# Prompt attention of a hybrid decoder step: scores with the keys on the partitions instead of the queries

## The chip, the cores and the metric

The kernel runs on one core of a Trainium2 chip. The metric is device microseconds (us) of one execution. TensorE (PE) multiplies, ScalarE (ACT), VectorE (DVE) and GpSimd (POOL) do the element-wise work, SyncE (SP) and POOL issue most DMAs. All arithmetic is on fp32 data; where a product needs full precision at the fast rate, an operand is split into a rounded high part (type fp32r) and a low part, and the product is made of several matmuls that add up in PSUM.

## The reference, cut to what matters

One decoder layer is computed for a prompt of 1024 tokens and for 8 samples of 8 tokens. Three head groups share one input projection: a sparse attention group (8 query heads, 2 KV heads, head size 64), a retention group, and a memory group (4 heads over 256 memory tokens). The change touches only the attention of the prompt:

```python
def masked_softmax(s, mask):
    s = jnp.where(mask, s.astype(jnp.float32), NEG_INF)
    m = jnp.max(s, axis=-1, keepdims=True)
    e = jnp.where(mask, jnp.exp(s - m), 0.0)
    return e / jnp.maximum(jnp.sum(e, axis=-1, keepdims=True), 1e-30)
...
    # per block of 128 queries and KV head (4 query heads each):
    s = jnp.einsum('bqkgd,bckd->bkgqc', q, kc) * SCALE      # compressed blocks (63 keys)
    s = jnp.einsum('bqkgd,bkqsd->bkgqs', qb, kg) * SCALE    # selected blocks (here all causal keys)
    s = jnp.einsum('bqkgd,bskd->bkgqs', qb, kw) * SCALE     # sliding window of 512 keys
    return gb[:, :, 0] * o_c + gb[:, :, 1] * o_s + gb[:, :, 2] * o_w
def mem_attend(q, mkv):
    s = jnp.einsum('bqhd,bmhd->bhqm', q, mkv[:, :, 0]) * SCALE
    p = jax.nn.softmax(s.astype(jnp.float32), axis=-1)
```

With 16 selected blocks of 64 keys and a prompt of 1024 tokens, the selected branch is plain causal attention. So a tile of 128 queries, number i (0 to 7), has i+1 key tiles of 128 in the selected branch, min(i+1, 5) in the window branch, one of compressed keys, and two of memory tokens.

## The kernel before, in words

The kernel has three stages on PE. The first projects the inputs (`pe_trunk`, lines 541 to 543) and slips compression, retention and the set-up of the attention between the projection jobs. The second is `pe_attend` with the prompt attention, into which the attention of the samples is slipped. The third (`project`, lines 1746 to 1748) multiplies the mixed heads by the output weights, a tile of 128 tokens at a time; its first step (lines 1742 and 1743, the samples) runs before the attention's last products.

The order of everything in the second stage is one list, made by `schedule()`, and each engine walks it in that order. Its unit v is one head of one query tile in one branch pair, `UNITS[v]`; there are 144. For a unit the list holds

- `qk`: PE adds the mask (line 1567, an identity by the mask, bf16) and the scores, with the queries as the stationary operand and the keys as the moving one: `QA` (high part of the queries, line 1575) and `QB` (low part, line 1576). The key tile `KS` has the keys' high part on the 64 partitions of its KV head and the low part on the other 64, and the queries stand on both halves, so the two matmuls give all four products. Scores lie in two pairs of PSUM banks, so `qk` of v waits for the exponentials of v-2 (line 1553);
- `max`: DVE reduces each row of scores to its negated maximum (line 1907);
- `sm`: ACT makes the exponentials with that maximum as bias and adds up each row (line 1839, two records: the operation and the read of its accumulator) into `P`;
- chunks `("p", ...)`: PE turns four tiles of 128 keys of `P` (line 1602, transposes) into one of three PSUM banks, 4, 5 and 6, which all small work shares in turn; ACT and DVE alternate in copying them to `PTs` (line 1772);
- `pv`: PE multiplies the values by `PTs` (line 1727), two heads of the two KV heads side by side, each on 64 columns of the array. An fp32 matmul leaves two records in the trace;
- `ot`, chunk `("o", ...)`, `norm`: ACT copies the output out of bank 7 (line 1863), PE turns it back (line 1607), DVE scales it by gate and sum (line 1929), POOL adds the branches (`pool_mix_group`).

Queries of later tiles are loaded by SP (`load_q`), turned by PE (line 1612), scaled by ACT or DVE into `qd` and split by POOL into `QA` and `QB` (lines 2142 and 2144). Chunks of the samples' attention (`sample_groups()`) follow one group to a unit. A chunk waits until the chunk three before it has been read (line 1592), since it takes its bank.

## Time and profile before

| | before |
|---|---|
| times of three runs, us | 970.45, 971.74, 973.53 (median 971.74) |
| span of the profiled execution, us | 970.0 |
| PE busy, share of the span | 96% |
| DVE, ACT, POOL busy, share of the span | 53%, 39%, 30% |
| granted TensorE clock, mean | 0.996 of full speed |
| PE records | 7997 |

The span runs from the first to the last instruction of the profiled execution, 1.7 us less than the median. A matmul's record is longer than the time it takes from the next one, since matmuls overlap in the array. What one costs is therefore read from the starts in the timeline, not from its duration.

### The profile page before, as it was taken

Reading aid. Unit: us, or ns where it says so; the run is one execution under the profiler, and the core shown is the slowest. Engines: PE = TensorE matmul, PEld = TensorE weight load, DVE = VectorE, ACT = ScalarE, POOL = GpSimd, SP = SyncE. Lnnn points to the kernel's source line nnn. Section 1 sums busy time; section 2 is a strip of 40 time slices with the busy share of each in tenths; the row PEclk is TensorE's granted clock in tenths of the full one; section 3 lists DMA queues with packets and bytes.
Section 4 is the critical chain, followed back from the end, with each engine's and each line's share of the span. In section 5 each row is a group of like instructions: output and inputs, shape, how many; then the busy total and the mean of one; then the engine's idle time right before and its main releaser. Section 6 shows DMA issues by size and latency. Waiting matters only on the chain.

```text
span 970.0 us, 20909 instructions
## 1 busy us (share of the span) xinstructions
PE 928.3 (96%) x7997; PEld 843.0 (87%) x7997; DVE 517.3 (53%) x1216; ACT 382.5 (39%) x973; POOL 289.1 (30%) x493
## 2 busy tenths in 40 slices
PE   4999999999999999999999999999999999999997
PEld 4999999999999999999988788878878888778885
DVE  6675322322222444337546677676777758944443
ACT  6333221224211012212456565656665657832221
POOL 0222222211216353462153153315311535310000
PEclk9999999999999999999999999999999999999998
DMA  7664404224242533322966156714504132424331
GB/s 242 157 218 117 158 20 170 84 100 118 69 142 83 134 127 100 104 82 60 226 191 146 36 155 240 240 44 123 167 2 126 56 103 73 134 98 134 132 133 69
DMA packets 97878, 119.16 MB, mean 123 GB/s; under 512 B 37763, under 2 KB 79779, under 8 KB 97203
## 3 DMA queue, kind: packets, MB, share of 16 engines
q1 hardware_dynamic: 84498, 74.41, 26.8%
q0 software_dynamic: 10224, 36.20, 11.0%
q10 hardware_dynamic: 3056, 7.21, 2.1%
q8 instruction: 65, 1.06, 0.5%
q14 instruction: 35, 0.28, 0.1%
HBM read 92.72 MB, written 32.02 MB: 129 GB/s over the span
## 4 chain that ended last, share of the span: by engine, by line
PE 78%; DVE 8%; issue 4%; DMA 4%; ACT 2%; POOL 2%; SPq 2%; DVEq 0%; ACTq 0%
PE psum L541 9%; PE psum L542 9%; PE psum L543 9%; PE psum L1727 7%; PE psum L1602 5%; PE psum L1575 3%; PE psum L1746 3%; PE psum L1747 3%; PE psum L1748 3%; PE psum L1576 3%; PE psum L770 2%; PE psum L772 2%; PE psum L771 2%; PE psum L753 2%; DMA r_rt<-in_c_rope 2%
## 5 line engine op out<-in xcount | busy, mean ns | idle before, releaser
L541 PE MATMUL psum<-a_whi,f_xhi 128*128 128x256 f32 (+1 forms) x864 | 250.9, 290 | 8.1 <-DVE f_xlo L959 4.4
L542 PE MATMUL psum<-a_wlo,f_xhi 128*128 128x256 f32 (+1 forms) x864 | 245.1, 284 | 0.0
L543 PE MATMUL psum<-a_whi,f_xlo 128*128 128x256 f32 (+1 forms) x864 | 244.3, 283 | 0.0
L541 PEld LDWEIGHTS psum<-a_whi,f_xhi 128*128 128x128 f32 x864 | 164.1, 190 | 11.9 <-issue 3.1
L543 PEld LDWEIGHTS psum<-a_whi,f_xlo 128*128 128x128 f32 x864 | 164.1, 190 | 0.0
L542 PEld LDWEIGHTS psum<-a_wlo,f_xhi 128*128 128x128 f32 x864 | 164.0, 190 | 0.0
L1907 DVE TENSOR_REDUCE p_nb<-psum 128x1 f32<-128x640 f32 (+7 forms) x224 | 110.4, 522 | 48.8 <-PE psum L1576 46.8
L1839 ACT ACTIVATE p_P<-psum,p_nb 128x640 f32<-128x640 f32 (+7 forms) x224 | 124.3, 562 | 25.9 <-DVE p_nb L1907 23.5
L685 POOL DMA_DIRECT2D h_scratch<-a_hst x117 | 64.1, 550 | 234.7 <-DVE a_hst L1015 146.4
L1602 PE MATMUL psum<-f_ident,p_P 128*128 128x128 f32 x656 | 101.8, 279 | 3.0 <-ACT p_qd L1852 1.4
L1602 PEld LDWEIGHTS psum<-f_ident,p_P 128*128 128x128 f32 x656 | 74.0, 140 | 8.6 <-ACT p_qd L1852 1.9
L1024 DVE TENSOR_TENSOR c_ctlo<-psum,c_cthi 128x512 fp32r<-128x512 f32 (+1 forms) x40 | 25.4, 636 | 101.1 <-ACT c_cthi L914 101.1
L1772 ACT COPY p_PT<-psum 128x512 f32<-128x512 f32 (+3 forms) x105 | 48.1, 458 | 66.1 <-PE psum L1602 65.3
L1727 PE MATMUL psum<-p_PT,p_V 128*64 128x128 f32 x1056 | 71.8, 279 | 1.5 <-DVE p_PT L1772 0.6
L1575 PE MATMUL psum<-p_KS,p_QA 128*128 128x320 f32 (+5 forms) x192 | 72.0, 378 | 0.0
L914 ACT CAST c_cthi<-psum 128x512 fp32r<-128x512 f32 (+1 forms) x40 | 21.8, 544 | 119.4 <-PE psum L753 119.4
L1727 PEld LDWEIGHTS psum<-p_PT,p_V 128*64 128x64 f32 x1056 | 56.4, 136 | 12.4 <-issue 9.5
L1772 DVE COPY p_PT<-psum 128x512 f32<-128x512 f32 (+3 forms) x111 | 64.5, 582 | 0.2
L1576 PE MATMUL psum<-p_KS,p_QB 128*128 128x320 f32 (+5 forms) x192 | 62.1, 327 | 0.0
L1746 PE MATMUL psum<-d_whi,d_xh 128*128 128x512 f32 x128 | 51.2, 400 | 0.0
L530 DVE TENSOR_TENSOR a_wlo<-a_wraw,a_whi 128x1024 fp32r<-128x1024 f32 (+1 forms) x30 | 37.7, 1294 | 24.8 <-ACT a_whi L523 24.7
L1747 PE MATMUL psum<-d_wlo,d_xh 128*128 128x512 f32 x128 | 50.6, 396 | 0.0
(317 smaller groups left out, 1836.6 us busy)
## 6 DMA issues: line engine op xcount, KB each, us to landing
a_wraw<-in_w_in SPq DMA_DIRECT2D x24, 512.0 KB, 4.9
h_scratch<-a_hst POOLq DMA_DIRECT2D x96, 128.0 KB, 2.6
s_SG<-in_cache_nsa_slc SPq DMA_DIRECT2D x64, 128.0 KB, 2.3
a_xraw<-in_x_prompt SPq DMA_DIRECT2D x8, 512.0 KB, 3.7
p_qd<-h_scratch SPq DMA_DIRECT2D x16, 256.0 KB, 4.0
s_MK<-in_cache_mem SPq DMA_DIRECT2D x8, 512.0 KB, 9.8
s_WG<-in_cache_nsa_win SPq DMA_DIRECT2D x8, 512.0 KB, 4.7
mix_scratch<-p_zt POOLq DMA_DIRECT2D x8, 512.0 KB, 3.8
```

Source lines behind the costliest of these rows:

```text
L541: nc.tensor.matmul(out, hi, wh, start=first, stop=False)
L542: nc.tensor.matmul(out, hi, wl, start=False, stop=False)
L543: return nc.tensor.matmul(out, lo, wh, start=False, stop=last)
L1575: nc.tensor.matmul(o, QA[par[i]][:, hq, :], k, start=at // 512 not in masked, stop=False, skip_group_check=True)
L1576: l = nc.tensor.matmul(o, QB[par[i]][:, hq, :], k, start=False, stop=True, skip_group_check=True)
L1602: l = nc.tensor.transpose(o[0:w, 128 * j:128 * j + 128], P[v % 2][:, at:at + w], ident[:])
L1727: i_mm = nc.tensor.matmul(psum[64 * j:64 * j + 64, at:at + 128], val, PTs[p_rank[pair[j]] % NPT][0:w, 128 * p:128 * p + 128], start=k == 0 ...
L1746: nc.tensor.matmul(o, hi, dwhi[jj][:, k], start=k == 0, stop=False)
L1747: nc.tensor.matmul(o, hi, dwlo[jj][:, k], start=False, stop=False)
L1772: copy(PTs[r % NPT][0:w, 0:128 * n], bank(4 + c % 3)[0:w, 0:128 * n]).then_inc(sem, 1)
L1839: nc.scalar.activation(dst, s_view(s), ACT.Exp, bias=nb[:, g % NNB:g % NNB + 1], accum_out=ssum[:, par[i], s[1]:s[1] + 1]).then_inc(S("p_e ...
L1907: nc.vector.tensor_reduce(out=nb[:, g % NNB:g % NNB + 1], in_=s_view(s), op=ALU.max, axis=AX.X if len(s[6]) == 1 else AX.XY, negate=True). ...
```

## The change

The unit of the attention stage becomes a block of one query tile and one KV head (16 blocks, `BLOCKS`), walked in the order of tiles 0, 2, 4, 6, 7, 5, 3, 1. For each block there are now two passes over the scores:

- a pass for the maxima alone, one block ahead: 9 units (`qk`, `max`), with masks as before and the `QA` matmuls alone. DVE reduces them into columns of `nbm`; chunk `("m", n)` turns `nbm` once, and ACT copies the rows of negated maxima into the unused half of the low part of the queries, `QB`, four copies;
- the scores themselves, turned: chunk `("s", n, b, k)` has 128 keys as the stationary operand and the 4 query heads (512 columns) as the moving one, `KS` by `QA` and then `KB` by `QB`. `KB` holds the keys' high part on one half and on the other half a constant that is one in the row of that branch's maximum. So the second matmul adds both the low part and the negated maximum. Where a mask is needed a third matmul adds it. ACT makes the exponentials from the shared bank straight into `PTs`, with no row sum. The transposes of `P`, `P` itself and the copies to `PTs` go.

The row sums come from the probabilities: POOL adds up the tiles of the selected branch (`A_s`), DVE those of the window branch (`A_w`), each add a 128x512 fp32 operation, and chunk `("u", n)` multiplies them by one-hot columns (`esel`), 20 products of 32 array columns each. Chunk `("v", n)` turns the result for DVE's weights. `pv` now takes 256 columns to a matmul instead of 128.

Queries are split by ACT and DVE straight from the bank, three deep. The memory layout moves: the values `V` and `VM` now lie where the projection's inputs were, so their load is issued after the projection has been stored, ahead of the loads of the third and fourth block's queries and of the samples' inputs; the masks are loaded first. In the set-up the keys are copied twice by ACT (`KS`, `KB`), and POOL fills `KB`'s constant rows. The output stage's weights are split in 8 pieces of 256 KB loads instead of 4 of 512 KB, and its residual rows and `gf` are loaded when the attention's last products are done.

```diff
-    PAIRS = [(6, 1), (7, 0), (5, 2), (4, 3)]
-    BLOCKS = [(pair[j], g) for pair in PAIRS for j, g in ((0, 0), (0, 1), (1, 0), (1, 1), (0, 2), (1, 2), (1, 3), (1, 4), (0, 3), (0, 4))]
+    TILES = [0, 2, 4, 6, 7, 5, 3, 1]
+    BLOCKS = [(i, kv) for i in TILES for kv in range(2)]
+    UNITS = [(n, l) for n in range(NB) for l in range(9)]
...
@@ def schedule():
+        for n in range(NB):
+            mine = score_chunks(n)
+            span = len(mine) - 2 if len(mine) >= 6 else len(mine) - 1
+            units = [list(range(9 * (n + 1) + 9 * k // span, 9 * (n + 1) + 9 * (k + 1) // span)) if n + 1 < NB and k < span else [] for k in range(len(mine))]
...
+            for k, c in enumerate(mine):
+                if k == len(mine) - 1 and n + 1 < NB:
+                    add(("m", n + 1))
+                pending.append(add(c))
+                due = [p for p in pending if p <= pending[-1] and len(pending) - pending.index(p) > 2]
+                if due and ends_phase(due[0]):
+                    products(1)
+                elif len(due) >= 2:
+                    products(2)
                 else:
+                    follow()
+                for v in units[k]:
+                    unit(v)
+                if n + 2 < NB and k in (1, 2):
+                    add(("q", n + 2, k - 1))
+                    if k == 2 and n + 4 < NB:
+                        steps.append(("load_q", n + 4))
...
@@ def sp_attend(sp):
-        load_q(sp, SECOND)
         wait_stored(sp, len(proj_jobs) - 1)
...
+        sp.dma_start(esel[:], io["c_esel"]).then_inc(S("p_esel"), 16)
+        for br, c in enumerate((C_KVS, C_KVW)):
+            sp.dma_start(V[:, br], hD[0:T, c + 128:c + 256].rearrange("(t p) n -> p t n", p=128)).then_inc(S("p_v"), 16)
+        sp.dma_start(VM[:], new_mem[:, 256:512].rearrange("(t p) n -> p t n", p=128)).then_inc(S("p_v"), 16)
+        load_q(sp, 2)
+        load_q(sp, 3)
...
@@ def qk(v):
-            if v >= 2:
-                pe.wait_ge(S("p_exp"), sm_count(v - 2))
+            else:
+                pe.wait_ge(S("p_nb"), max_count(v - 2))
...
-                    nc.tensor.matmul(o, QA[par[i]][:, hq, :], k, start=at // 512 not in masked, stop=False, skip_group_check=True)
-                    l = nc.tensor.matmul(o, QB[par[i]][:, hq, :], k, start=False, stop=True, skip_group_check=True)
-            l.then_inc(S("p_qk"), 1)
+                    r = nc.tensor.matmul(psum[:, at:at + w], QA[n % 3][:, hq, :], k, start=at // 512 not in masked, stop=True, skip_group_check=True)
+            r.then_inc(S("p_qk"), 1)
+
+        def scores(c, o):
...
+            if (b, k) == (0, 0):
+                wait_queries(pe, n)
+                wait_chunk_read(pe, place["m", n])
+            if b == 3:
+                for hh in range(2):
+                    for m in range(2):
+                        om, keys = o[:, 128 * (2 * hh + m):128 * (2 * hh + m) + 128], slice(128 * m, 128 * m + 128)
+                        nc.tensor.matmul(om, KM[:, kv + 2 * hh, keys], qa[:, 4 + hh, :], start=hh + m == 0, stop=False, skip_group_check=True)
+                        l = nc.tensor.matmul(om, KMB[:, kv + 2 * hh, keys], qb[:, 4 + hh, :], start=False, stop=True, skip_group_check=True)
+                return l
...
+            og = o.rearrange("p (g q) -> p g q", g=4)
+            if m_at is not None:
+                nc.tensor.matmul(og, maskb[:, m_at:m_at + 128], identb[:].rearrange("p (o q) -> p o q", o=1).to_broadcast([128, 4, 128]), start=True, stop=False)
+            nc.tensor.matmul(og, ka, qa[:, 0:4, :], start=m_at is None, stop=False)
+            return nc.tensor.matmul(og, kb, qb[:, 0:4, :], start=False, stop=True)
+
+        def sums(n, o):
...
+            for b in range(4):
+                p = (A_s, A_w)[b] if b < 2 and summed(n, b) else probs(chunk_of(n, b, first_key(i, b)))
+                for m in range(2 if b == 3 else 1):
+                    for t in range(4):
+                        at = 256 * (t % 2) + 128 * m if b == 3 else 128 * (2 * (t % 2) + t // 2)
+                        l = nc.tensor.matmul(o[32 * t:32 * t + 32, 0:128], esel[:, 32 * b:32 * b + 32], p[:, at:at + 128],
+                                             start=b == 0, stop=b == 3 and m == 1, skip_group_check=True)
...
@@ def act_attend(act):
+                if kind[0] == "s":
+                    act.wait_ge(S("p_tr"), n + 1)
+                    if s_rank[n] >= NPT:
+                        wait_probs_read(act, s_index[s_rank[n] - NPT])
+                    nc.scalar.activation(probs(n)[:], o, ACT.Exp).then_inc(S("pt_act"), 1)
+                elif kind[0] == "m":
...
+                    rows = slice(64 - 64 * kv, 68 - 64 * kv)
+                    for g in range(4):
+                        src = psum[32 * g:32 * g + 4, 512 * (4 + n % 3):512 * (4 + n % 3) + 128]
+                        if g < 2:
+                            k = nc.scalar.copy(QB[m % 3][rows, g::4, :], src.rearrange("p (o q) -> p o q", o=1).to_broadcast([4, 2, 128]))
+                        else:
+                            k = nc.scalar.copy(QB[m % 3][rows, g, :], src)
```

## Rows read from the trace of the kernel before

**Rows 1.** The page's part 1: busy time, share of the span, records.
```profile
PE 928.3 (96%) x7997; PEld 843.0 (87%) x7997; DVE 517.3 (53%) x1216; ACT 382.5 (39%) x973; POOL 289.1 (30%) x493
```

**Rows 2.** Windows, the three stages: length, busy (records) by engine, clock, DMA.
```profile
0.00:489.00 489.00, 467.88 (x3905) 457.17 (x3906) 205.56 (x477) 125.62 (x233) 146.34 (x240) 1.00 0.42 125
489.00:867.00 378.00, 364.48 (x3654) 307.95 (x3654) 267.25 (x623) 233.83 (x680) 135.84 (x241) 1.00 0.41 122
867.00:970.00 103.00, 95.95 (x442) 77.92 (x441) 44.51 (x116) 23.00 (x60) 6.88 (x13) 0.98 0.32 115
```

**Rows 3.** Lines of PE from 489 to 867 us: busy, mean ns | idle before.
```profile
L1602 PE MATMUL psum<-f_ident,p_P 128*128 128x128 f32 x656 | 101.8, 279 | 3.0 <-ACT p_qd L1852 1.4 <-DVE p_PT L1772 1.0 <-ACT s_PTS L1790 0.4
L1575 PE MATMUL psum<-p_KS,p_QA 128*128 128x320 f32 (+5 forms) x192 | 72.0, 378 | 0.0
L1727 PE MATMUL psum<-p_PT,p_V 128*64 128x128 f32 x1056 | 71.8, 279 | 1.5 <-DVE p_PT L1772 0.6 <-issue 0.6
L1576 PE MATMUL psum<-p_KS,p_QB 128*128 128x320 f32 (+5 forms) x192 | 62.1, 327 | 0.0
```

**Rows 4.** Timeline of PE at 558 us: start, us, line, form, records.
```profile
558.03 0.45 PE L1575 MATMUL psum<-p_KS,p_QA 128*128 128x448 f32 x1
558.31 0.36 PE L1576 MATMUL psum<-p_KS,p_QB 128*128 128x448 f32 x1
558.51 0.37 PE L1575 MATMUL psum<-p_KS,p_QA 128*128 128x448 f32 x1
...
558.92 0.60 PE L1602 MATMUL psum<-f_ident,p_P 128*128 128x128 f32 x4
559.45 0.66 PE L1727 MATMUL psum<-p_PT,p_V 128*64 128x128 f32 x8
559.94 0.39 PE L1727 MATMUL psum<-p_PT,f_VC 128*64 128x128 f32 x4
560.26 0.66 PE L1612 MATMUL psum<-f_ident,p_qd 128*128 128x128 f32 x4
```

**Rows 5.** Timeline of PE in the output stage.
```profile
899.80 0.40 PE L1746 MATMUL psum<-d_whi,d_xh 128*128 128x512 f32 x1
900.03 0.39 PE L1747 MATMUL psum<-d_wlo,d_xh 128*128 128x512 f32 x1
```

**Rows 6.** Timeline of PE, products on 32 array columns, and what follows.
```profile
553.80 0.40 PE L1650 MATMUL psum<-s_MK,s_PTM 128*32 128x256 f32 x4
554.13 0.39 PE L1575 MATMUL psum<-p_KM,p_QA 128*128 128x256 f32 x1
```

**Rows 7.** Lines of ACT, DVE and POOL (489 to 867 us; the first two from 640 us).
```profile
L1839 ACT ACTIVATE p_P<-psum,p_nb 128x512 f32<-128x512 f32 x16 | 11.1, 693 | 1.9 <-DVE p_nb L1907 1.9
L1772 ACT COPY p_PT<-psum 128x256 f32<-128x256 f32 x19 | 7.1, 372 | 13.8 <-PE psum L1602 13.7
L1839 ACT ACTIVATE p_P<-psum,p_nb 128x640 f32<-128x640 f32 (+7 forms) x224 | 124.3, 562 | 25.9 <-DVE p_nb L1907 23.5 <-PE psum L1602 0.8 <-PE psum L1581 0.6
L1907 DVE TENSOR_REDUCE p_nb<-psum 128x1 f32<-128x640 f32 (+7 forms) x224 | 110.4, 522 | 48.8 <-PE psum L1576 46.8 <-ACT p_P L1839 0.7
L1772 DVE COPY p_PT<-psum 128x512 f32<-128x512 f32 (+3 forms) x111 | 64.5, 582 | 0.2
L2037 DVE TENSOR_TENSOR d_wlo<-d_wraw,d_whi 128x1024 fp32r<-128x1024 f32 x8 | 10.6, 1319 | 0.2 <-ACT d_whi L1883 0.2
L2144 POOL TENSOR_TENSOR p_QB<-p_qd,p_QA 128x512 fp32r<-128x512 f32 x21 | 26.8, 1277 | 1.7
```

**Rows 8.** Set-up and start: key copies, first exponential, query loads (KB, us to landing).
```profile
L950 ACT CAST p_KS<-psum x8: 579/582/585, 466.8 to 473.3; 64x512 fp32r<-64x512 f32 x8
...
494.35 0.99 ACT L1839 ACTIVATE p_P<-psum,p_nb 128x896 f32<-128x896 f32 x1
...
p_qd<-h_scratch SPq DMA_DIRECT2D x8, 256.0 KB, 5.0
```

**Rows 9.** Source of line 2088, a POOL addition: ns min/median/max.
```profile
L2088 POOL TENSOR_TENSOR p_Oi<-p_Oi x32: 452/457/1394, 514.1 to 867.4; 128x128 f32<-128x128 f32 x32
```

More of the change, by code:

```diff
@@ new lines, in follow @@
+        def follow():
+            if queue:
+                c = queue.pop(0)
+                add(c)
+                if c[0] == "o" and c[2] == 1:
+                    steps.append(("norm", c[1]))
+                    i, kv = BLOCKS[c[1]]
+                    if kv == 1:
+                        nxt = TILES.index(i) + 2
+                        if nxt < QT:
+                            timed.append([2, ("load_z", TILES[nxt])])
+                            timed.append([6, ("gates", TILES[nxt])])
@@ L1369, in schedule @@
             if d == 0:
-                while waiting:
-                    pv()
-                while outs:
-                    write(outs.pop(0)[0])
+                while pending:
+                    products(2 if len(pending) >= 2 and not ends_phase(pending[0]) else 1)
+                while queue:
+                    follow()
+                steps.extend([("load_x", 0), ("load_x", 1)])
             if d + 2 < NT:
@@ L1910, in weights @@
[L1910 to L1913 removed]
+            if l == 0 and n >= 1:
+                dve.wait_ge(S("p_tr"), place["m", n - 1] + 1)
+            for b, g, _, views in maxes(v):
+                nc.vector.tensor_reduce(out=nbm[:, 32 * g + b:32 * g + b + 1], in_=max_view(views), op=ALU.max, axis=AX.X if len(views) == 1 else AX.XY,
+                                        negate=True).then_inc(S("p_nb"), 1)
```

851 lines of the change are left out of this document (444 added, 407 removed).

## The prediction

> **What bounds the kernel now.** Read the busy shares first [rows 1]: PE is busy 96% of the span, DVE 53%, ACT 39%, POOL 30%. Then the windows by stage [rows 2]: the change acts on the middle one, 489 to 867 us, where PE is busy 364.5 of 378 us at the full clock (1.00) while DVE has 267, ACT 234 and POOL 136. So the stage is set by the number and form of matmuls, and at most 13.5 us of it is idle time that a better order could give back. A lighter DVE or ACT gives nothing beyond that. The lines of PE [rows 3] show what the change touches: transposes of P (656), score matmuls (192 wide ones by QA, as many by QB), values (1056 records of V). Their durations overlap, so prices come from the distance of starts.
>
> **Prices.** In [rows 4] a QB matmul of 448 columns takes 558.51 - 558.31 = 0.20 us, a QA of as many columns behind a mask 0.28, four transposes 0.53 before the value products begin and value records of 128 columns 0.49 for eight. With 0.11 for a transpose (4 x 0.11 = 0.44) that leaves 0.09 for the change of form into value products; the last four records take 0.32 against some 0.22 to 0.24, so 0.10 for the change back. In [rows 5] a matmul of 512 columns takes 0.233 us, its stationary operand's load hidden. In [rows 6] four records on 32 columns each of the array, 256 wide, take 0.33 us with the change of form, 0.23 without: they run side by side.
>
> **Removed from PE.**
> - QB in the score pass: 288 matmuls. 192 for V's branches and 32 for memory have 75,800 columns (528 x 128 + 32 x 256), at 0.20/448 us each 34 us. 64 compressed ones are only 64 wide; they can't be shorter than the load of a stationary operand, for which I take the transpose's 0.11: 7 us. Together 41 us.
> - 656 transposes x 0.11 = 72 us.
> - Value products: columns stay the same (two matmuls of 256 for four of 128), so 0 (bounds: -5 from fewer records, +3). They come in about 84 groups plus 16 of sums instead of 116; 16 fewer changes of form x 0.19 = 3 us less.
>
> **Added to PE.**
> - Turned scores. The number of chunks: selected branch 36, window 30, compressed and memory 8 each, times two KV heads = 164. 148 of them are two matmuls of 512 columns: 148 x 0.466 = 69 us. The 16 memory chunks are eight matmuls of 128 columns with a stationary operand each, 0.11 apiece: 14 us. 56 chunks have a mask (16 + 16 diagonals, 8 window tails, 16 compressed), 512 columns of it: 56 x 0.233 = 13 us. Entering the form: between 0 and 0.08 a chunk (0.28 against 0.20 in [rows 4]), half the chunks follow work of the same form; I take 4 us of at most 13.
> - Sums: 20 fp32 products a block are 40 records, ten sets of four. A set of 256 columns takes 0.23 [rows 6]; at 128 columns half of it, 0.12, is what the array rate leaves, 0.23 the other bound. With 0.2 for changes of form 16 x 1.4 = 22 us (bounds 18 and 40).
> - 32 transposes of maxima and sums: 4 us.
> - The pass of the maxima keeps masks and QA: no change.
>
> Added 69 + 14 + 13 + 4 + 22 + 4 = 126, removed 41 + 72 + 3 = 116: **PE's own work grows by 10 us** (bounds -5 and +35). The transposes' saving is eaten because the score products are now made one and a half times and the sums are PE's.
>
> **The other engines.** ACT: before 234 us; after, 164 exponentials x 0.69 (128x512 in [rows 7], without the accumulator reads) = 113, four copies a block at 0.37 = 24, output and query copies 34, sums 4, the rest some 35 as now: 210. DVE: 267 - 65 (copies to PTs) - 7 + 44 window adds at half of 1.32 us, 29 + query splits 15 = 240; the 224 maxima stay [rows 7]. POOL: 136 - 40 (splits) + 56 adds x 1.28 [rows 7] = 72 + 7 for wider mixing = 175. All far below PE's some 385, so they are hidden as long as their order holds. PE now never waits for a maximum before an exponential, since that lies a block ahead, and probabilities reach the values three chunks later. Of the 13.5 us idle I take 10 as given back (bounds: all of it, and 15 us more than before).
>
> **The start.** Three things are exposed there.
> - Set-up: ACT makes ten more key copies at 0.58 us [rows 8], 5.8 us inside some three projection jobs, with evictions queued behind them that PE needs four jobs later, and the key loads now land behind the mask's. Cover: the projection. I take 2 us (0 to 5).
> - First block: nothing can be scored until nine units are reduced (14 reduces, some 4 us), turned, copied four times (1.5 us). The first exponential, at 494.35 [rows 8] today, comes some 6.5 us later. In these 6.5 us PE has the units' 2.5 us of matmuls, which are not extra work, and about 1 us of idle time that it has today as well; 3 us are new (1 to 5).
> - The third block's queries are turned one chunk after the first scores, but SP issues their load behind V and VM (1.25 MB), and only when the projection is stored. A load of queries lands 5.0 us after its issue [rows 8]. PE stops at that chunk, and all chunks are behind it: 4 us (0 to 9).
>
> Nine us together. The values load is needed later than these queries and hides. The late load of residual rows has the second output step, 48 x 0.233 = 11 us, as cover; if it were gone it would cost the load's 5 us. The query loads of later blocks have two blocks of cover.
>
> **The sum.** Span 970.0 + 10 - 10 + 9 = 979. The median of the runs is 1.7 us over the span of the profiled execution, so 980.7 us.
>
> **Rivals.**
> 1. *The order heals it.* The added side work is small beside what ACT and DVE lose (65 us of copies, 45 of accumulator reads), so all 13.5 idle us go; forms of matmul cost nothing to enter (-4), value records gain 5, and the queries land in time, leaving 3 us at the start. For it: PE's idle gaps end mostly at ACT and DVE. Against: a stage with 96% of PE already busy. 970 + 10 - 13.5 - 4 - 5 + 3 = 960.5, 962 us measured. Chance 0.27.
> 2. *ACT becomes the pace at the block seams (slower still).* Every score bank is now read by ACT alone, out of three shared banks, and at each seam ACT has the four copies of maxima (1.5 us) before the next block's scores may start, with output, sum and query copies queued in the same place. It decides once ACT's queue at a seam exceeds the one score chunk and value pair that PE has there (0.9 + 0.5 us). Price 1.3 us x 16 on top of the forecast: 20 us, 1000 us. Speaks against it that ACT has only 210 us in 164 chunks, 1.3 us for PE's 2.3. A relative of it: a POOL addition usually takes 0.46 us but once 1.39 [rows 9], so POOL can be held up threefold, and its adds free the probability buffers. If each of the 44 window adds held or was held for one POOL add, 44 x 1.28 = 56 us would fall on DVE, which has 138 us free, so by itself it moves nothing. Chance 0.12 for both. The Trainium skill (SBUF — State Buffer, section Who interferes with whom) says that DVE and GpSimd share one pair of SBUF ports under an exclusive lock, which a DVE operation with two SBUF inputs takes. The trace's 1394 ns against 457 agrees with such a lock.
> 3. *The products on 32 columns don't overlap.* Then 40 records at the 0.11 of a lone one instead of 1.2 us a set of ten: 16 x 3.2 = 51 us more, 1030 us. [Rows 6] speaks against. Then the sums would not be the cheap step that the change takes them for. Chance 0.03.
> 4. *A wash:* more of the idle time given back and the queries on time: 968.8 to 974.7. Chance 0.10.
>
> **How the numbers follow.** The forecast has 0.48, with its own range 975 to 992 from the bounds of the start (1 to 19), of the sums and of the idle time. Two in ten lie outside 958 to 1000: the tail of rival 1 and the upper half of rivals 2 and 3. A change under 0.3% (2.9 us) can't be told from none: faster 0.27 (rival 1), same 0.10 (rival 4), slower 0.48 + 0.12 + 0.03 = 0.63.
>
> **What the profile after would show.** PE's records of line 1602's kind gone; score chunks with starts 0.23 apart, 0.47 a chunk; the sums' forty records in 1.2 to 1.4 us; POOL over 170 us and DVE near 240 in the stage. PE idle at the first blocks, with a query load as releaser. Wrong would be: a stage shorter than 378 us with the same start (the count of work or the idle share is off), or PE waiting for ACT at each seam (rival 2), or a projection that ends more than 5 us later than today (set-up underestimated).

## The result, and the profile after

The changed kernel takes 1031.03 us (median; 1028.28 to 1037.42) against 971.49 us before (970.45 to 973.53): ratio 1.062, 95% interval 1.059 to 1.066. The forecast was 980.7 us with a range of 958 to 1000: the sign was right, the size far off, and the range too narrow. The profiled execution has a span of 1028.4 us, 58.4 more than before. From the page of the kernel after, the parts that answer [rows 1], and the clock by slices of 25.7 us:

```profile
span 1028.4 us, 19390 instructions
PE 949.8 (92%) x7613; PEld 798.0 (78%) x7613; DVE 511.2 (50%) x1116; ACT 339.5 (33%) x681; POOL 326.6 (32%) x503
PE   4999999999999999989799939999999979999997
PEclk9999999999999999999799969999999999999999
```

One execution differs from the next by several us (the longest and shortest here by 9), so differences of a few us between single executions below are followed to their place in the trace.

PE's busy share fell from 96% to 92%, and three places stand out: slices 20, 24 and 33 (about 500, 600 and 835 us). The windows of the kernel after (length, busy us by engine, then clock, DMA share, GB/s): first the three stages, as [rows 2], then the two conspicuous stretches of the middle one, and last one that is undisturbed.

```profile
0.00:489.00 489.00, 465.01 (x3884) 454.15 (x3885) 206.50 (x478) 129.81 (x243) 151.06 (x245) 1.00 0.41 121
489.00:925.00 436.00, 389.30 (x3296) 266.60 (x3294) 259.51 (x521) 187.19 (x379) 167.98 (x245) 0.95 0.37 108
925.00:1028.00 103.00, 95.50 (x436) 77.26 (x436) 45.23 (x117) 22.51 (x59) 7.53 (x13) 0.99 0.35 124
600.00:640.00 40.00, 26.77 (x192) 17.61 (x193) 14.30 (x23) 12.36 (x26) 10.34 (x19) 0.76 0.43 138
820.00:860.00 40.00, 31.77 (x236) 19.95 (x229) 35.14 (x41) 20.70 (x37) 27.84 (x26) 0.91 0.39 100
640.00:820.00 180.00, 172.43 (x1489) 116.23 (x1492) 114.15 (x230) 81.47 (x166) 65.99 (x81) 0.99 0.33 96
```

The output stage is as long as before. The attention stage grew from 378 to 436 us. The other engines came out near the forecast: ACT 187 (forecast 210), DVE 260 (240), POOL 168 (175). But in the undisturbed 180 us PE is busy 96%, as before; its idle share didn't shrink. And the two stretches hold waits that the forecast didn't have.

**Around 600 us.** PE's wait with its releaser (us in total, times, longest):

```profile
PE psum L1802 <- DMA s_SG<-in_cache_nsa_slc: 16.0, 1, 16.0
```

Line 1802 turns the keys of a pair of samples. Their sixteen pages are loaded by SP (s_SG); the timeline of SP and ACT in the kernel after has the loads and what ACT issues among them:

```profile
575.36 17.85 SPq L1553 DMA_DIRECT2D s_SG<-in_cache_nsa_slc  x16
594.29 14.07 SPq L658 DMA_DIRECT2D p_qd<-h_scratch  x1
586.79 1.33 ACTq L1993 DMA_DIRECT2D out_new_win_s<-in_cache_nsa_win  x1
```

ACT starts the 4 MB copy of the window cache at 586.79, while SP issues pages from 575.36 to 593.21. The issue of one query load behind them takes 14.07 us. Before, the issue of the pages was over (556.21 + 17.86 = 574.07) ten microseconds ahead of the copy. The copy held a query load then as well, for 16.61 us, but PE waited for none of it:

```profile
556.21 17.86 SPq L1467 DMA_DIRECT2D s_SG<-in_cache_nsa_slc  x16
584.67 1.34 ACTq L1865 DMA_DIRECT2D out_new_win_s<-in_cache_nsa_win  x1
590.92 16.61 SPq L646 DMA_DIRECT2D p_qd<-h_scratch  x1
```

The schedule places both by count: the loads at its 25th unit and the copy at the 36th before, at the 23rd and 30th chunk after. The window's keys of the same pair are issued at 554.26 before and 573.40 after, the copy at 584.67 and 586.79: the distance shrank from 30.4 to 13.4 us, and the loads take 20. The lines of the change that do it, not in the cut of the diff shown above:

```diff
-        first = 8
...
-            for what, n in groups.pop(0) if v >= first and groups else []:
...
-            if v == 36:
-                steps.append(("copy_win", 0))
...
+                if slot >= 6 and groups:
+                    for what, m in groups.pop(0):
...
+                if slot == 30:
+                    steps.append(("copy_win", 0))
```

**Around 840 us.** DVE is busy 35.1 of 40 us and POOL 27.8. POOL waits 10.6 us for the samples' reloaded results and then mixes them in one piece of 10 us (824.13 to 834.1), with additions for the sums queued behind it. DVE has the eight splits of the output weights there. The spread of their durations, kernel before and then after (ns min/median/max):

```profile
L2037 DVE TENSOR_TENSOR d_wlo<-d_wraw,d_whi x8: 1210/1222/1820, 815.8 to 846.6; 128x1024 fp32r<-128x1024 f32 x8
```

```profile
L2172 DVE TENSOR_TENSOR d_wlo<-d_wraw,d_whi x8: 1225/2152/3775, 819.2 to 854.3; 128x1024 fp32r<-128x1024 f32 x8
```

The longest of the eight starts just behind the first operation of POOL's mixing and ends 1.1 us after it (POOL ends at 826.94, DVE at 828.02):

```profile
824.13 2.81 POOL L2309 TENSOR_TENSOR s_on_s<-s_on_s,s_gs 64x1536 f32<-64x1536 f32 x1 [10.59 <-DMA s_om_s<-om_scratch]
824.25 3.77 DVE L2172 TENSOR_TENSOR d_wlo<-d_wraw,d_whi 128x1024 fp32r<-128x1024 f32 x1
```

**At the start.** Before, PE was busy 27.07 of the 29 us from 491 at the full clock; after, 18.33 of the 26 us from 494, at 0.74 (windows of the kernel before, then after):

```profile
491.00:520.00 29.00, 27.07 (x274) 24.25 (x274) 19.07 (x37) 19.26 (x52) 16.92 (x41) 1.00 0.85 243
```

```profile
494.00:520.00 26.00, 18.33 (x100) 12.96 (x101) 10.70 (x36) 8.84 (x19) 10.23 (x38) 0.74 0.84 233
```

The projection's last matmul starts at 493.81 (before 491.29), then PE waits 0.85 us for the maxima, 1.5 for ACT's copies of them and 2.65 for the third block's queries.

### The profile page after: what moved, and what is told of

The parts are those of the page before. It is cut to its first block, busy times and chain, and to the rows that moved or that the text cites. A ratio compares the mean times of both kernels' runs of the same rounds, so it can differ in the third digit from the quotient of the medians.

```text
span 1028.4 us, 19390 instructions
## 1 busy us (share of the span) xinstructions
PE 949.8 (92%) x7613; PEld 798.0 (78%) x7613; DVE 511.2 (50%) x1116; ACT 339.5 (33%) x681; POOL 326.6 (32%) x503
## 4 chain that ended last, share of the span: by engine, by line
PE 70%; DMA 8%; DVE 8%; SPq 4%; POOL 3%; issue 3%; ACT 2%; DVEq 0%; POOLq 0%
PE psum L555 8%; PE psum L556 8%; PE psum L557 8%; PE psum L1868 5%; PE psum L1889 3%; PE psum L1888 3%; PE psum L1887 3%; PE psum L1672 3%; PE psum L1701 2%; DMA s_SG<-in_cache_nsa_slc 2%; PE psum L1702 2%; PE psum L796 2%; DVE p_nbm L2036 2%; PE psum L798 2%; PE psum L797 2%
## 5 line engine op out<-in xcount | busy, mean ns | idle before, releaser
L2036 DVE TENSOR_REDUCE p_nbm<-psum 128x1 f32<-128x640 f32 (+7 forms) x224 | 108.8, 522 | 82.7 <-PE psum L1672 81.1
L1956 ACT ACTIVATE p_PT<-psum 128x512 f32<-128x512 f32 x164 | 97.2, 597 | 124.2 <-PE psum L1702 118.4
L1868 PE MATMUL psum<-p_PT,s_V 128*64 128x256 f32 x528 | 73.1, 397 | 0.0
L1701 PE MATMUL psum<-p_QA,p_KS 128*128 128x512 f32 x132 | 68.7, 521 | 3.0 <-ACT p_PT L1956 1.4
L1508 POOL TENSOR_TENSOR p_A_s<-p_A_s,p_PT 128x512 f32<-128x512 f32 x42 | 55.6, 1324 | 22.1 <-ACT p_PT L1956 20.0
L1702 PE MATMUL psum<-p_QB,p_KB 128*128 128x512 f32 x132 | 53.5, 405 | 0.0
L1887 PE MATMUL psum<-d_whi,d_kh 128*128 128x512 f32 x128 | 51.1, 399 | 0.0
L544 DVE TENSOR_TENSOR a_wlo<-a_wraw,a_whi 128x1024 fp32r<-128x1024 f32 (+1 forms) x30 | 38.3, 1313 | 24.8 <-ACT a_whi L537 24.6
L1889 PE MATMUL psum<-d_whi,d_bh 128*128 128x512 f32 x128 | 50.6, 395 | 0.0
L1888 PE MATMUL psum<-d_wlo,d_kh 128*128 128x512 f32 x128 | 50.6, 395 | 0.0
L796 PE MATMUL psum<-c_cthi,c_w1hi 128*128 128x256 f32 (+2 forms) x160 | 47.5, 297 | 0.5 <-DVE c_ctlo L1064 0.4
```

The source lines that it names most:

```text
L1701: nc.tensor.matmul(og, ka, qa[:, 0:4, :], start=m_at is None, stop=False)
L1702: return nc.tensor.matmul(og, kb, qb[:, 0:4, :], start=False, stop=True)
L1868: mm = nc.tensor.matmul(psum[64 * j:64 * j + 64, at:at + 256], val, probs(c)[:, 256 * j:256 * j + 256], start=first, stop=b == 2 or k == i ...
L1887: nc.tensor.matmul(o, hi, dwhi[jj][:, k], start=k == 0, stop=False)
L1888: nc.tensor.matmul(o, hi, dwlo[jj][:, k], start=False, stop=False)
L1889: l = nc.tensor.matmul(o, lo, dwhi[jj][:, k], start=False, stop=k == KT - 1)
```

## The experiments

The theory after the first reading: PE's work is near the forecast, and the rest is the copy ahead of the pages, the start, and the burst on DVE and POOL near 840 us. The rivals: page loads that are late by themselves, a clock that costs time of its own, blocks of few keys, and a pass of maxima that costs more than its matmuls. Spans of profiled executions are compared, since a place can be followed in them. PE walks one fixed list, so the start of the same matmul in two kernels shows where a difference arises; the matmul of line 1702 that closes the compressed chunk of a block serves as a mark.

**Each suspect alone.** Copies later: `slot == 30` and `36` become 35 and 41.

> The changed kernel with its copies of the window cache (4 MB, from DRAM to DRAM) and of the new keys and values issued five slots of the schedule later, nothing else. In the changed kernel the large copy is issued at 586.8 us, in the middle of the sixteen page loads of the first pair of samples (575.4 to 593.2), and PE then waits 16.0 us for a page, with its granted clock at 0.76 between 600 and 640. Theory A: the copy fills the DMA queues ahead of the last pages. Then the wait of line 1802 for the pages falls from 16.9 to under 2 us, the clock of that stretch returns to 0.97 or more, and the span falls from 1028.4 to about 1008 (1005 to 1012). Theory B: the pages are late because SP issues them late, behind its waits, whatever ACT copies. Then the wait stays above 12 us and the span above 1022.

Span 1009.9 us (-18.5). The wait of 16 us is gone (0.6 us at a page is left), and the clock of the stretch is back:

```profile
600.00:640.00 40.00, 38.00 (x364) 25.93 (x361) 23.83 (x47) 18.39 (x38) 10.14 (x14) 1.00 0.61 214
```

Theory A. The gain sits in this place: from the mark of the fifth block to that of the sixth it takes 29.15 us, and 47.64 in the changed kernel. ACT now issues the copy at 600.43, behind the last page (594.3). It still holds a query load, for 9.83 us at 610.86, and PE doesn't wait for it.

Queries first:

```diff
+        load_q(sp, 2)
+        load_q(sp, 3)
         sp.dma_start(esel[:], io["c_esel"]).then_inc(S("p_esel"), 16)
         for br, c in enumerate((C_KVS, C_KVW)):
```

> The changed kernel with the loads of the third and fourth block's queries issued by SP ahead of those of the one-hot columns and of the values (they were behind them), nothing else. In the changed kernel PE waits 2.65 us for them at 510 us, at a granted clock of 0.50 between 500 and 510. Theory A (the prediction's term for this, 4 us, now with its clock): the queries land before PE turns them, PE's wait for the query load is gone, and the span falls by 3 to 5 us, to 1023 to 1026. Theory B: the values are then what is late, since they are loaded behind the queries: PE waits for them at the first value products by 2 us or more and the span falls by under 1 us.

Span 1024.1 (-4.3), the wait for the queries gone. But the first score chunk was already 1.4 us early from the projection, where executions differ by that much (its last matmul starts between 491.97 and 494.79 in these runs), so the move itself gives some 1.3 to 3 us (1.3 from the projection's last matmul to the mark of the second block). Theory A in kind, at half its size or less.

Waits filled with matmuls (`fill(o, n)`: n times identb x maskb[:, 0:512] into the bank written next):

> The changed kernel with useless matmuls of 512 columns in bf16 in the three waits of PE at the start of the attention stage: 4 ahead of the turning of the first maxima (0.9 us), 7 ahead of the first scores (1.5 us), 12 ahead of the third block's queries (2.7 us). Their results are overwritten before anybody reads them. It keeps the waits as long as they are and takes away only PE's inactivity. Theory A: the granted clock of 0.50 between 500 and 510 us comes from these waits and costs time of its own. Then the clock stays at 0.95 or more and the span falls by 3 to 6 us. Theory B: PE is waiting in this stretch anyway, so a higher clock only lengthens the waits: the span stays within 1.5 us of 1028.4.

Span 1027.2 (-1.2), and the clock did what was wanted:

```profile
500.00:510.00 10.00, 8.89 (x45) 4.54 (x44) 2.37 (x10) 2.43 (x6) 6.83 (x27) 0.93 1.15 298
```

PE goes on at 510.02, where it went on at 509.99 in the kernel after: both times when the queries land. Theory B: at a clock of 0.50 (all at 1.2 GHz) PE only reached the same transfer with less waiting. At this place nothing was gained (from the projection's last matmul to the mark of the second block 31.0 us, 30.8 in the changed kernel), and the 1.2 us of the span arose elsewhere. DMA's busy share, the last column but one, is 1.15 in this window, which fits a stretch that waits for transfers.

Weights on three slots: `groups += [[w_hi], [w_lo, load_w], []]`.

> The changed kernel with the eight splits of the output weights (ACT makes the high part, DVE the low part of 1024 columns in 1.4 us alone and 2.0 to 3.8 us beside POOL) on three slots of the schedule each instead of two, nothing else. In the changed kernel DVE is busy 17.3 of 20 us between 840 and 860 and PE only 14.0, PE waits 3.1 us there for the last maxima of a block, and its clock falls to 0.83. Theory A: DVE is the pace between 820 and 860, because the splits, the window's additions and the maxima meet there. Spreading gives 3 to 7 us, span 1021 to 1025. Theory B: the blocks of few keys are the cause by themselves (nine units of maxima to four or six chunks), whatever DVE does beside them: the loss stays, span within 1.5 us of 1028.4.

Span 1032.3 (+3.9). Theory A as stated fell: DVE is relieved (10.6 of the 20 us from 840), but PE isn't. The start of this execution is 3.9 us later by itself, so the spreading is worth nothing, rather than harmful. What the waits from 836 to 864 us name instead is POOL:

```profile
ACT p_PT L1956 <- POOL p_A_s L1508: 10.6, 3, 6.0
```

An exponential needs a probability buffer that POOL's addition has yet to read. In the changed kernel this wait is 3.0 us in all, so the spreading itself has lengthened it.

This execution also bears on the price of the slow clock. All engines' work is the same as in the changed kernel up to the splits, but the clock is 0.50 for 30.7 us at the start instead of 13.7, and from the projection's last matmul (491.97) to the mark of the third block (551.34) it takes 59.4 us instead of 53.6 (493.81 to 547.41).

**Both transfers moved**, the base of what follows but one:

> The changed kernel with the two moves of transfers together: the large copies five slots later, and the queries of blocks three and four loaded ahead of the values. Alone they gave 18.5 us (the window copy) and 4.3 us (the queries). Theory A: the two act at different places (590 to 613 us, and 500 to 512 us) and add up, to a span of 1028.4 - 18.5 - 4.3 = 1005.6 us, 1003 to 1009. Theory B: they are the same slack counted twice, since what is gained at the start moves the page loads towards the copy again: then the sum is under 20 us and the span over 1009.

1008.69 us (1006.34 to 1012.35), ratio 1.039 (1.036 to 1.043); span 1009.1. The profiled span is just over the line between the theories, but the spans of the four executions run from 1004.5 to 1010.5, so the line can't be drawn with it. By place the two add up: the copies' 18.5 us are there, and the queries' move gives 0.7 us to the mark of the second block (1.3 where it stood alone). In this execution 1.6 us are lost again near 754 us, in a stretch of 3.4 us at a clock of 0.50 that the execution with the copies alone hasn't; so the spans differ by 0.8 only.

**POOL's piece cut in five** (`fin` as five steps, one a slot, from the sixth slot behind `load_fin`; then from the eleventh, the weights four slots later; then from the sixth, the weights four slots later):

> The kernel with both moves of transfers, and with POOL's mixing of the samples' results, which is one piece of 10 us behind a wait of 10.6 us for reloaded data, cut into five pieces in five consecutive slots of the schedule, the first four slots later than now. Theory A: this one piece on POOL is what holds up the additions for sums between 820 and 860 us; the additions free the probability buffers, ACT's exponentials wait for them (1.7 to 6.0 us at a time in the runs so far), PE waits for the exponentials and its clock falls to 0.83. Then the 7 to 10 us lost there shrink to under 4, and the span is 1005.6 - 5 = 1000 us (997 to 1003). Theory B: it is DVE, with the splits of the output weights, that sets the pace there; POOL's order is nothing: within 1.5 us of the kernel with both moves.

> As the one before, but with POOL's five pieces another five slots later, where the block at work adds nothing on POOL (its window branch, whose additions are DVE's), and the splits of the weights four slots later. Theory A (POOL is what holds it up): as good as the kernel before or better, 995 to 1002 us. Theory B (DVE is the pace): the splits now fall wholly into the blocks of few keys, as in the run that spread them, and the span is 2 to 5 us over that of the kernel with both moves, 1008 to 1011.

> The kernel with both moves of transfers, POOL's mixing of the samples in five pieces in consecutive slots as before, and the splits of the output weights four slots later. In the two runs with pieces DVE waited 5.6 and 7.9 us for the samples' store, which the fifth split of the weights needs (the store came later than the split), and the maxima queued behind it; here the store is in time. Theory A: POOL's single piece was a real cause and the two runs with pieces only bought a new wait. Then DVE's wait for that store is gone and the loss between 800 and 860 us falls from 11 us to under 6: span 1000 to 1004. Theory B: POOL's piece isn't the cause: the loss stays, 1006 to 1012.

Spans 1014.6, 1014.0 and 1008.3. The first lost (median 1013.76, ratio 1.044, 1.042 to 1.046); the second can't be told from its base by its median (1010.29, ratio 1.040, 1.038 to 1.041). From the mark of the eleventh block to that of the last the two take 96.9 and 95.9 us, the base 92.9. This comes by a wait that the cutting made: DVE stood 5.6 and 7.9 us at a split whose buffer lies over the samples' data, with the next block's maxima behind it. With the splits later that wait is gone, and nothing is gained (93.1). Moved like this, the work costs as much.

**Work left out**, to tell the two engines apart:

> The kernel with both moves of transfers, with the low parts of the output weights set to zero by DVE in place of the subtraction (this leaves out the low part of the output weights; a plain write of 128x1024 instead of 1.4 to 3.8 us). Theory A (DVE is the pace between 800 and 860 us): the 11 us lost there shrink to under 5: span 1001 to 1004. Theory B (POOL's sample mixing ahead of the additions): they stay, within 2 us of 1009.1.

> The kernel with both moves of transfers, with POOL's mixing of the samples' results left out except for its waits and its store (so 10 us of POOL's work between 805 and 816 us are gone, and the samples' output is wrong). Theory A (POOL's piece holds up the additions, and through the probability buffers ACT and PE): the 11 us lost between 800 and 860 us shrink to under 5: span 1001 to 1004. Theory B (DVE): they stay, within 2 us of 1009.1.

> The kernel with both moves of transfers, with the low parts of the output weights set to zero and POOL's mixing of the samples left out (the output weights' low part and the samples' output are not computed). One alone took 6 us off, the other 4. If these two are the whole cause of what is lost between 800 and 860 us, under 2 of the 11 us remain and the span is 998 to 1000. If blocks of few keys lose time by themselves, 4 us or more remain: 1001 to 1004.

Spans 1003.0 (-6.1), 1005.3 (-3.8), 998.4 (-10.7). The same 40 us in the kernel with both moves and in the last of these (called h4 below):

```profile
800.00:840.00 40.00, 32.27 (x255) 20.31 (x252) 34.99 (x40) 21.55 (x39) 27.84 (x26) 0.91 0.37 101
```

```profile
800.00:840.00 40.00, 36.73 (x263) 23.40 (x263) 27.38 (x50) 23.04 (x42) 18.71 (x25) 0.96 0.34 104
```

These spans overstate it, because all engines' work is the same up to the first split of the weights, and the last kernel is 4 us ahead there already. The marks of the eleventh and of the last block, in the kernel with both moves and in the one without both pieces of work:

```profile
794.93 0.40 PE L1702 MATMUL psum<-p_QB,s_KCB 128*128 128x512 f32 x1
887.84 0.39 PE L1702 MATMUL psum<-p_QB,s_KCB 128*128 128x512 f32 x1
```

```profile
790.75 0.40 PE L1702 MATMUL psum<-p_QB,s_KCB 128*128 128x512 f32 x1
877.18 0.39 PE L1702 MATMUL psum<-p_QB,s_KCB 128*128 128x512 f32 x1
```

Between them lie 92.9 and 86.4 us: leaving out both is worth 6.5 us. The other 4.2 us arose ahead of the work left out, where the clock is 0.50 for 20.5 us in the one execution and 10.2 in the other; they are the execution's, not the work's. DVE's work alone gives 1.8 us in this stretch (91.1) and POOL's alone 3.0 (89.9). The kernels that have all the work there in its place (the changed one and five of its variants) take 91.4 to 94.4, so DVE's share alone isn't clear of that spread, POOL's just is, and both together are. So it is both, at 6.5 us and not 11.

Thinning out both gave nothing:

> The kernel with both moves of transfers, with POOL's sample mixing in five pieces and the splits of the output weights on three slots each: both causes found between 800 and 860 us thinned out at once, and the samples' store ahead of the fifth split. Leaving out the low parts of the weights took 6 us off, leaving out POOL's mixing 4. Theory A (the two queues together, in bursts): spreading both recovers at least half of the 11 us, span 1001 to 1004. Theory B (the amount of work on DVE and POOL in this stretch, not its bursts, is what is short): spreading moves the loss and recovers under 2 us, 1007 to 1010.

1009.37 us (1005.24 to 1011.43), ratio 1.039 (1.035 to 1.043), span 1009.6: the outcome of theory B. But in its trace ACT waits 9.3 us for POOL's additions, against 3.0 in the kernel with both moves, and PE 5.3 us at once for a copy of ACT's, so the holds moved. That the amount of work on DVE and POOL is short, rather than its order, is argued and not shown.

**Large tiles there instead:** `TILES = [0, 2, 3, 5, 4, 6, 7, 1]`.

> The kernel with both moves of transfers, with the tiles of queries taken in the order 0, 2, 3, 5, 4, 6, 7, 1 in place of 0, 2, 4, 6, 7, 5, 3, 1, so that the large tiles 6 and 7 are at work while POOL mixes the samples and ACT and DVE split the output weights. Theory C: what is lost between 800 and 860 us is lost because the side work meets blocks of few keys, whose maxima, copies and additions come densest; with large blocks there, under 4 of the 11 us remain, and the small tile 3, now early, costs under 2: span 1001 to 1005. Theory A or B alone (the side work blocks a queue whatever block it meets): the loss stays, 1007 or more.

Span 1012.5 (+3.4): theory C fell, and the profile shows POOL's hold in one piece. Timeline of ACT, PE and POOL of this kernel; the number in brackets is the idle time before:

```profile
806.65 3.08 POOL L2309 TENSOR_TENSOR s_on_s<-s_on_s,s_gs 64x1536 f32<-64x1536 f32 x1 [4.99 <-DMA s_om_s<-om_scratch]
...
814.70 1.25 POOL L2208 TENSOR_TENSOR s_zs<-s_on_s,s_zs 64x512 f32<-64x512 f32 x1
...
816.83 1.27 POOL L1508 TENSOR_TENSOR p_A_s<-p_A_s,p_PT 128x512 f32<-128x512 f32 x1
818.20 0.66 PE L1717 MATMUL psum<-p_A_s,p_esel 128*32 128x128 f32 x8 [8.69 <-issue]
818.21 0.60 ACT L1956 ACTIVATE p_PT<-psum 128x512 f32<-128x512 f32 x1 [9.94 <-POOL p_A_s L1508]
```

Ten microseconds of mixing, one addition behind them, and ACT and PE stand until it is done.

**The first block not awaited** (its zero shift is turned after two of nine units; its maxima are still computed):

> The kernel with both moves of transfers, where the first block's maxima are computed as before but not awaited: its exponentials subtract zero (no protection against overflow in that block, sums held above 1e-30). PE turns the zero maxima after two units of the nine, so ACT's copies run beside the other seven. Theory A (the prediction's term of the first block: 3 us of waits for reductions and copies, and the clock that falls with them): the first scores come 2.4 us or more earlier relative to the end of the projection, and the loss between 480 and 520 us falls from 13 to 7 or less: span 1002 to 1006. Theory B: the start hangs on the third block's queries, which land when they land: under 2 us, span over 1007.

Span 1010.2 (+1.1). The maxima are off the path, and PE waits at the values in their place:

```profile
PE psum L1872 <- DMA s_VM<-out_new_mem: 2.1, 1, 2.1
```

Theory B's outcome with another cause than it named. The first scores come 2.4 us earlier after the projection, and by the mark of the third block all of it is lost again. The DMA busy shares of 1.11 and 1.04 in the windows from 500 and 510 us and the wait for the values speak for a start that is bound by what must land; the clock of 0.50 for 17 us at the start is in the same stretch, and no run tells the two apart here.

**The pass of the maxima.** From the third block on, `unit(v)` is left out and zero subtracted; then the same with the transfers cleared (copies twelve slots later, three more slots ahead of each pair's pages).

> The changed kernel without the pass of the maxima from the third block on: those blocks subtract zero ahead of the exponential in place of the maximum (the same ratio of sums, but without protection against overflow). This leaves out 14 of 16 blocks' score matmuls for maxima with their masks, and DVE's reductions for them. Nothing else is moved, so the page loads' wait of 16 us may stay. Theory A: PE's amount of work sets the time outside the few long waits. The pass has 67 us of PE's distances of starts in the changed kernel, some 62 of them in these blocks: span 1028.4 - 62 = 966 us (960 to 974). Theory B: with so much less of PE's work, the exponentials and the additions at 1.3 us a chunk on POOL and DVE become the pace, and the copies collide earlier: span over 980.

> The kernel that subtracts zero in place of the maxima from the third block on (it leaves out the maxima of 14 blocks), now with both moves of transfers, the large copies twelve slots later and three more slots between a pair's window keys and its pages, so that no page is awaited. Without these it had a span of 999.3 us, with 27.3 us of waiting for pages. Theory A: the pass of the maxima costs what its matmuls take, some 62 us, and only the waits for pages hid that: span 999.3 - 27 - 3 = 969 us (962 to 976). Theory B: with the pass gone the path from scores over exponential and addition to values is the pace between the transfers, so the pass filled time that PE would wait anyway: span 980 or more, with PE's waits for ACT's exponentials and POOL's additions above 20 us.

Span 999.3: only 29 us for 62 us of matmuls, with 27.3 us of PE's waits for pages. Cleared:

```profile
PE psum L1805 <- DMA s_SG<-in_cache_nsa_slc: 2.7, 1, 2.7
```

959.66 us (958.30 to 963.03), ratio 0.990 (0.986 to 0.994), span 956.5. By the medians this is 49 us under the kernel with both moves (the spans, the shortest of four here against a long one there, say 53), and 1% under the kernel before. Theory A in kind, with a span 5.5 us under its range. Part of the 49 us may not be PE's, since DVE's reductions for these blocks go as well; no run separates the two. The first run's theory B held only in that transfers ate much of the gain. This kernel has no protection against overflow in 14 blocks, so it is a price, not a replacement; the kernel before wasn't run without its maxima.

## Why the prediction was wrong, point by point

- **PE's work** (+10): right, to about a microsecond (worked out below). What the trace shows of the terms: forty records of sums take 1.23 us in 14 of the 16 blocks (forecast 1.4 with changes of form), so rival 3 is out. Of two score chunks in a row each takes 0.56 to 0.57 us. A chunk with a mask, from the mask's start to the next work, takes 0.68 here:

```profile
677.93 0.38 PE L1700 MATMUL psum<-f_identb,p_maskb 128*128 128x512 bf16 x1
677.96 0.58 PE L1701 MATMUL psum<-p_QA,s_KCp 128*128 128x512 f32 x1
678.38 0.40 PE L1702 MATMUL psum<-p_QB,s_KCB 128*128 128x512 f32 x1
678.61 0.60 PE L1802 MATMUL psum<-f_ident,s_SG 128*128 128x128 f32 x4
...
682.38 0.50 PE L1701 MATMUL psum<-p_QA,p_KS 128*128 128x512 f32 x1
682.71 0.40 PE L1702 MATMUL psum<-p_QB,p_KB 128*128 128x512 f32 x1
682.95 0.39 PE L1701 MATMUL psum<-p_QA,p_KS 128*128 128x512 f32 x1
683.18 0.40 PE L1702 MATMUL psum<-p_QB,p_KB 128*128 128x512 f32 x1
683.51 0.65 PE L1868 MATMUL psum<-p_PT,f_VC 128*64 128x256 f32 x4
```

  The forecast had 0.466, 0.233 for a mask, and 4 us in all for entering the form, 86 us for the 148 chunks. Most chunks stand alone, between units, transposes and values. Outside the slow clock the starts of 85 chunks without a mask give a mean of 0.59 us (0.46 to 0.67) and of 49 with one 0.74, some 96 us for all, so entering and leaving the form was nearer the bound of 13 than 4. The 656 transposes, priced at 72 us without their changes of form, were worth more too (some 86 us by their starts), and the two errors nearly cancel.
- **The start** (+9): low by some 4 us, inside its bounds. Set-up took 2.5 for 2. From 494 to 520 us PE is busy 18.33 of 26 us at a clock of 0.74, so it loses 7.7 idle and about 18.33 x 0.26 = 4.8 to the clock; 1.9 of that was there before. That is some 10.5 for 7, and the clock wasn't a term of the forecast. In h4, which has the queries first and none of the causes below, the same sum gives 5.4 + 4.1 - 1.9 = 7.6. The sentence "the values load is needed later than these queries and hides" held: with the queries first PE waits for no values. Only with the first block's maxima not awaited as well does it wait 2.1 us for them.
- **The idle time** (-10): the wrong step. None was given back. From the projection's last matmul to the output stage (kernel before, changed kernel and h4; columns as above):

```profile
491.29:867.00 375.71, 362.19 (x3635) 305.66 (x3634) 267.25 (x623) 233.45 (x679) 135.30 (x240) 1.00 0.41 122
493.81:925.00 431.19, 384.49 (x3255) 261.79 (x3253) 259.51 (x521) 186.43 (x377) 166.90 (x243) 0.95 0.38 109
494.70:895.40 400.70, 377.17 (x3255) 258.26 (x3253) 246.57 (x522) 186.38 (x377) 155.73 (x237) 0.98 0.40 118
```

  PE is idle 13.5 us before and 46.7 after, 33 more, where the forecast had 10 less and 15 more as the bound (the new waits at the start, 7 us, were priced apart). Even in h4 it is idle 23.5 us, 10 more than before: 3.5 of these at the start, the rest in small waits, most of 0.1 to 0.9 us (for a copy, a split of queries, a maximum), the longest of 1.9. DVE and ACT are lighter there from 520 to 900 us (240 and 177 us busy), so how busy they are isn't what sets these gaps; that it is how close a step stands to the one that it needs is argued from these waits, not tested.
- **"All far below PE's some 385, so they are hidden as long as their order holds"**: the order didn't hold, at two places that could be read from the change and the trace of before. One is the copy and the pages (18.5 us): in the schedule's counts they came from eleven apart to seven, and by the clock the loads came 19 us later and the copy 2. By the schedule the slots of the small first blocks, which carry nine units each of the next, are the long ones. The prediction looked at SP's query loads and never set the copy against the pages. The other is POOL (with DVE 6.5 us): its wait for the samples' data and the mixing behind it cost nothing while nobody needed POOL; with the additions behind it, it holds the probability buffers. Rival 2 had this path ("its adds free the probability buffers") and was given 0.12, as an average over the stage: 175 of 385 us. The place counted, not the sum: at [rows 7]'s price the splits take 1.3 us of DVE, here 2.15 and up to 3.8. ACT at the seams, that rival's main mechanism, was not it.

The sum again, from the rows above. The changed kernel's span is 58.4 us longer: 2.5 for the projection's end, 22.3 of PE's busy time, 33.2 of idle time, and 0.4 of rounding. Its clock was 0.50 for 44.4 us of this stretch, in which PE was busy 24.6 us; half of that, 12.3, is an estimate of what the slow clock added to the busy time, and 10.0 are left for PE's work, as forecast. In h4 it is 3.4 + 15.0 + 10.0 = 28.4, with some 5.5 of the 15.0 from the clock, so 9.5 for PE's work. The 30 us between the two are 18.5 (copy), 6.5 (DVE and POOL), 0.8 (queries) and 4.2 that are the executions' own.

So the step that failed is the idle time, held to be covered "as long as their order holds": the order broke at two places, of 18.5 and 6.5 us, the small waits grew instead of shrinking, and the slow clock that came with the waits had no term. The bound of the idle time, "15 us more than before", was drawn for all waits together, and the wait for the pages alone passed it. The observation named for a wrong forecast, "PE waiting for ACT at each seam", didn't appear; a stage as long as 436 us had no entry at all.

## What to carry to other kernels

When a change alters what a schedule's slot lasts, write down by the clock when each large transfer, each reload and each piece of side work now falls, and compare the order between queues with that of before; a count that is nearly the same may stand for another time. When an engine gets new work, look for the longest single piece and the longest wait that already stand in its queue, since an average share says nothing of them. And a pass of matmuls that fills gaps is priced by leaving it out twice, as it stands and with the transfers cleared: here 29 us and 49 us for the same 62. And before a difference of a few microseconds between two executions is given to an edit, look whether it arises where the edit is.

## What the runs showed of the hardware

- A 4 MB copy from DRAM to DRAM, issued on ACT's queue, held a query load of SP for 14.07 us at its issue and the last pages for some 16 us. Issued 14 us later it still held a query load for 9.83 us, and in the kernel before for 16.61, and PE waited for neither: what such a copy costs depends on what is issued behind it. The Trainium skill (DMA: Bandwidth & Descriptors, section Queues, rings and completion order) says that each DMA engine goes round the queue rows a whole packet at a time. The trace agrees as far as it goes, in that the other queue's loads neither stopped for good nor kept their pace; the length of a packet isn't shown by a run here.
- DVE's subtraction of 128x1024 has a median of 1222 ns where POOL rarely works beside it and 2152 ns beside POOL's additions and mixing. The longest, 3775 ns, started 0.12 us behind a POOL operation of 2.81 us and ended 1.1 us after it. With POOL's mixing left out the median is 1351 ns, against 2156 in the kernel with both moves. The Trainium skill (SBUF — State Buffer, section Who interferes with whom) has the two engines share one pair of ports under an exclusive lock. The trace agrees, now from DVE's side: DVE is held up by POOL, not only POOL by DVE.
- A granted clock of 0.50 over 10 us cost nothing that could be seen where the next thing on the path was a transfer (the filled waits). It isn't free in general: 17 us more of it at the start went with 5.8 us more for the same instructions (the spread weights).
- Executions of one kernel differ in their mean clock and in their time with it. The four of the kernel with both moves have 0.983 (spans 1009.1 and 1010.5) or 0.988 (1004.5 and 1004.7).
